# A 31-tap depthwise convolution moved wholly to TensorE: four time shifts stacked over the partitions, eight rounds of four 32-column products for each tile

## The chip, the cores and the metric

One core of one Trainium2 chip. The metric is the device time of the whole program in microseconds, median of three runs. A profile of one further execution gives every instruction of the core; all times below count from the start of its span.

## The reference, cut to what matters

The program is two networks in a row: two layers of a first block, then four layers of a second one. The change touches one part of one layer, the convolution module that opens the second network. It works on 256 tokens (T) and 1024 channels (D):

```python
def causal_dwconv(x, w, b):                      # w: 31 taps x 1024 channels
    xp = jnp.pad(x, ((0, 0), (width - 1, 0), (0, 0)))
    ...                                          # each channel with its own 31 taps
    return y + b

def conformer_conv_module(h, w_pw1, b_pw1, dw_w, dw_b, ln_g, ln_b, w_pw2, b_pw2):
    # u = GLU(h @ w_pw1 + b_pw1)
    u = causal_dwconv(u, dw_w, dw_b)
    # layer norm over the channels, silu, @ w_pw2 + b_pw2
```

All of it is float32.

## The kernel before, in words

Channels lie on the 128 partitions and time along the free axis, so 1024 channels are eight tiles (KD) of 128 x 256. The function `conformer` builds the stage.

**The projection.** `project` computes h @ w_pw1 on TensorE (PE). Each weight block of 128 x 128 takes three products (lines 761, 762, 763), because both operands are split in a rounded upper part and a rest. Step m of the eight steps makes the two tiles (value and gate) of output tile m: 16 blocks, 48 products. Steps 0 and 1 are made together at the start (`open_step`). Weights come as units of 1 MB through a ring of six units, loaded by SyncE (SP, line 494, called from `Weights.refill`), which waits until a unit has been used. ScalarE (ACT, line 563) rounds each chunk of weights and VectorE (DVE, line 572) subtracts to get the rest. `act_step` and `dve_step` do that some chunks ahead.

**The gate.** When step m is done, ACT evicts the value (line 2608) and the sigmoid of the gate (2609), and DVE multiplies them into `u[:, m]` and raises `glu_ready` (2653).

**The convolution.** Tiles 3, 5 and 7 are convolved on PE: 31 products for each tile, one for a tap, with a 128 x 128 diagonal matrix of that tap's weights as the stationary operand and the shifted window of `u` as the moving one (line 2674, plain float32: two records in the trace for each product). ACT makes these 93 diagonals (line 2612) and takes the finished tile out of PSUM (`take`, line 2598, signal `conv_taken`). Tiles 0, 1, 2, 4 and 6 are convolved on DVE, one instruction for a tap and tile (lines 2627 and 2629, 155 in all), between its pieces of weight work and, what is left, after the last gate.

**What follows.** `statistics` sums the eight tiles on PE with a matrix of ones (line 2688, `mean_ready`). DVE subtracts the mean (line 2662), ACT squares (2621), PE sums the squares (2692). Just ahead of that, ACT splits one more chunk of weights for the next projection and loads a table (lines 563 and 816), and DVE takes the rest of that chunk (572).

**Elsewhere in the program** stand products whose stationary operand has fewer than 128 columns. Lines 2960, 2961 and 2962 issue, in turn, products of 96, 64 and 32 moving columns, each with a 128 x 32 stationary block and each to another group of 32 PSUM partitions. Lines 1950 and 1953 issue products with 64 stationary columns to alternate halves of the PSUM partitions, two on one half, then two on the other. All are plain float32.

Of the kernel before, what the change touches and what calls it, by code (L numbers as in the profile page):

```python
# [13 lines left out]
ALU = mybir.AluOpType  # L14
ACT = mybir.ActivationFunctionType
AX = mybir.AxisListType

P = 128
T = 256
NT = T // P  # L20
D = 1024
KD = D // P
# [43 lines left out]
ARENA_CUTS = (8192, 16384, 26624)  # L66
BANK = 512

MAGIC = 12582912.0
# [244 lines left out]
def parameter_columns():  # L314
    c = Columns()
# [22 lines left out]
    c.add("b_pw1", "cc_b_pw1_2", (0,), 2 * KD)  # L338
    c.add("dw_w", "cc_dw_w_2", (0,), TAPS_CC * KD)
    c.add("dw_b", "cc_dw_b_2", (0,), KD)  # L340
# [20 lines left out]
def shape_constants():  # L361
# [8 lines left out]
        "right_angle": np.where((p >= D_NOPE) & (p < D_QK), np.pi / 2, 0.0),  # L370
        "ident": p == f,
        "heads": p // D_RW == f // D_RW,
        "causal_add": np.concatenate([np.zeros((P, P)), np.where(f <= p, 0.0, NEG)], 1),
# [289 lines left out]
def over(ap, n):  # L663

    ap = ap.unsqueeze(1)
    return ap.broadcast_to([ap.shape[0], n] + list(ap.shape[2:]))
# [14 lines left out]
def project(chip, st, name, nk, epilogue, x=None, rhs=None, per=1, x_ready=None, entry=None, after=None, free=None,  # L681
            inserts=None, depth=None):

# [16 lines left out]
    @block.sync  # L700
    def _(sp):
        w.refill(sp, chip.groups[name])

# [1834 lines left out]
def conformer(chip, i):  # L2538
# [6 lines left out]
    xs = chip.x[:, :].rearrange("p (c t) -> p c t", t=T)  # L2545
    pad = TAPS_CC - 1
    u = chip.place(4 * SLOT, KD, pad + T)
    conv, plain = chip.place(6 * SLOT, KD, T), slot2(chip, 12)
    squares, rstd = slot2(chip, 3), chip.stat[:, 3 * T:4 * T]
    e = [chip.place(7 * SLOT + b * T, T) for b in range(2)]  # L2550
    on_pe, on_dve = (3, 5, 7), ((0, 1), (2, 4), (6,))
    taps_of = lambda tiles: [(m, n) for m in tiles for n in range(TAPS_CC)]
    pe_taps = taps_of(on_pe)
    diagonals_by = (4, 8, 14, 20, 38, 56, 75, len(pe_taps))
    n_first = 2 * SLOT // P
    first, rest = chip.place(SLOT, n_first, P), chip.place(7 * SLOT + 2 * T, len(pe_taps) - n_first, P)
    diagonal = lambda c: first[:, c, :] if c < n_first else rest[:, c - n_first, :]
    tap = lambda m, n: chip.col("dw_w", n * KD + m)
    conv_bank = lambda c: chip.bank(6 + c % 2, T)
    half = TAPS_CC // 2  # L2560
    w = chip.weights

    with fused(chip) as st:
        whole_ready, upper_ready, lower_ready, glu_ready, conv_ready, conv_taken, diagonals_ready, taps_done, mean_ready, \
            centred, squared, var_ready, root_ready = st.signals(
                "whole_ready", "x_upper_ready", "x_lower_ready", "glu_ready", "conv_ready", "conv_taken", "diagonals_ready",
                "taps_done", "mean_ready", "centred", "squared", "var_ready", "root_ready")

# [21 lines left out]
        def glu(block, s, banks, steps):  # L2590

            @block.scalar
            def _(act):
                made = taken = 0

                def take(c):
                    act.wait_ge(conv_ready, c + 1)
                    act.activation(conv[:, on_pe[c], :], conv_bank(c), ACT.Identity,
                                   bias=chip.col("dw_b", on_pe[c])).then_inc(conv_taken, 1)

                for m in range(KD):
                    s["act_step"](act, m)
                    if m == 7:
                        take(0)
                    act.wait_ge(s["ready"], s["through"](m))
                    if m >= 2:
                        act.wait_ge(glu_ready, m - 1)
                    act.activation(u[:, m, pad:pad + T], banks(m)[0], ACT.Identity, bias=chip.col("b_pw1", m))
                    act.activation(e[m % 2], banks(m)[1], ACT.Sigmoid,
                                   bias=chip.col("b_pw1", KD + m)).then_inc(s["free"], 1)  # L2610
                    for tile, n in pe_taps[made:diagonals_by[m]]:
                        act.activation(diagonal(made), chip.con("ident"), ACT.Identity,
                                       scale=tap(tile, n)).then_inc(diagonals_ready, 1)
                        made += 1
                for c in range(1, len(on_pe)):
                    take(c)
                w.act(act, s["last"])
                load_roots(act)
                for k in range(KD):
                    act.wait_ge(centred, k + 1)  # L2620
                    act.activation(squares[:, k, :], conv[:, k, :], ACT.Square, scale=1.0 / 32).then_inc(squared, 1)
                act.wait_ge(var_ready, 1)
                root_of(chip, act, rstd, chip.bank(1, T), LN_EPS, root_ready)

            def convolve(dve, m, n):
                if n == 0:
                    return dve.tensor_scalar(conv[:, m, :], u[:, m, 0:T], tap(m, 0), chip.col("dw_b", m),
                                             ALU.mult, ALU.add)
                return dve.scalar_tensor_tensor(conv[:, m, :], u[:, m, n:n + T], tap(m, n), conv[:, m, :],  # L2629
                                                ALU.mult, ALU.add)  # L2630

            @block.vector
            def _(dve):
                chain = Chain(dve, s["dve_chain"])
                todo = [(m, n, pair) for pair in on_dve for n in range(TAPS_CC) for m in pair]
                state = {"taps": 0, "glus": 0}

                def take_taps(count):

                    for m, n, pair in todo[state["taps"]:state["taps"] + count]:  # L2640
                        if pair[-1] >= state["glus"]:
                            return
                        if n:
                            dve.wait_ge(taps_done, state["taps"] - len(pair) + 1)
                        convolve(dve, m, n).then_inc(taps_done, 1)
                        state["taps"] += 1

                w.between = lambda dve, c: take_taps(3 if state["glus"] < 4 else 9)
                dve.memset(u[:, :, 0:pad], 0.0)
                for m in range(KD):  # L2650
                    s["dve_step"](dve, m)
                    dve.wait_ge(s["free"], m + 1)
                    chain(dve.tensor_tensor(u[:, m, pad:pad + T], u[:, m, pad:pad + T], e[m % 2], ALU.mult), glu_ready)  # L2653
                    state["glus"] += 1
                w.between = lambda dve, c: None
                take_taps(len(todo))
                dve.wait_ge(taps_done, len(todo))
                w.dve(dve, s["last"])
                dve.wait_ge(conv_taken, len(on_pe))
                dve.wait_ge(mean_ready, 1)  # L2660
# [4 lines left out]

        def taps(pe, start, count):
            for c in range(start, start + count):
                m, n = pe_taps[c]
                if n == 0:
                    pe.wait_ge(glu_ready, m + 1)  # L2670
                    if c // TAPS_CC >= 2:
                        pe.wait_ge(conv_taken, c // TAPS_CC - 1)
                pe.wait_ge(diagonals_ready, c + 1)
                ins = pe.matmul(conv_bank(c // TAPS_CC), diagonal(c), u[:, m, n:n + T], start=(n == 0),  # L2674
                                stop=(n == TAPS_CC - 1))
                if n == TAPS_CC - 1:
                    ins.then_inc(conv_ready, 1)

        def statistics(pe):
            taps(pe, TAPS_CC + half, 2 * TAPS_CC - half)  # L2680
            ones = chip.con("ones")
            order = [m for pair in on_dve for m in pair] + list(on_pe)
            for k, m in enumerate(order):
                if m in on_pe:
                    pe.wait_ge(conv_taken, on_pe.index(m) + 1)
                else:
                    pe.wait_ge(taps_done, TAPS_CC * (k // 2 * 2 + len(on_dve[k // 2])))
                ins = pe.matmul(chip.bank(0, T), ones, conv[:, m, :], start=(k == 0), stop=(k == KD - 1))
            ins.then_inc(mean_ready, 1)
            for k in range(KD):  # L2690
# [3 lines left out]

        project(chip, st, ("pw1", i), KD, glu, per=2, x=h, x_ready=lower_ready, after=statistics, depth=3,
                inserts={10: lambda pe: taps(pe, 0, half), 12: lambda pe: taps(pe, half, TAPS_CC - half),
                         14: lambda pe: taps(pe, TAPS_CC, half)})

# [1126 lines left out]
```

## Time and profile before

| | |
|---|---|
| median of three runs | 2506.34 us (2505.02 to 2508.89) |
| the profiled execution's own time | 2506.61 us |
| its span, first to last instruction | 2504.8 us |
| mean granted TensorE clock | 0.971 |
| TensorE / VectorE / ScalarE busy over the span | 93% / 78% / 58% |
| the stage: first product of the projection to first subtraction of the mean | 976.3 to 1082.3 us |

The profile names a group of instructions by line, engine and operation, with the tile written, the tiles read and their shapes. The time an engine sat idle is put down to the instruction that ended it. A TensorE record's duration holds the latency of its pipeline, so the rate of products is read from starts, not from durations.

### The profile page before, as it was taken

The numbers are of one execution on the slowest core, as the hardware profiler recorded it, in microseconds if no ns is written. First come the engines' busy times: TensorE is split into PE (matmuls) and PEld (weight loads), VectorE is DVE, ScalarE is ACT, GpSimd is POOL, SyncE is SP. The second block draws the span as 40 slices with busy tenths as digits, with TensorE's granted clock in tenths as the row PEclk, the third lists the DMA queues.
The fourth block names the chain that finished last, engine by engine and source line by source line (L and its number), as shares of the span: only waits on it lengthen the run. The fifth ranks groups of instructions, "written<-read, shape, count | busy, mean of one in ns | idle before, by whom it ended". The sixth has DMA issues, their size and how long they took to land. (4 is left out here: it accounts for less than half of the span.)

```text
span 2504.8 us, 45660 instructions
## 1 busy us (share of the span) xinstructions
PE 2330.6 (93%) x18410; PEld 2221.1 (89%) x18410; DVE 1947.6 (78%) x3438; ACT 1447.1 (58%) x2673; POOL 12.8 (1%) x20
## 2 busy tenths in 40 slices
PE   8899999989999998889998979999988999988998
PEld 7899999978999998779997979997787999866998
DVE  6578798766688976968888868896559889857885
ACT  7535565465365645657746667656454775534764
POOL 0000000000000000000000000000000000000000
PEclk9999999999999999999999989999998999989999
DMA  6215577723175786214585525573425457722552
GB/s 248 89 52 203 189 285 299 303 85 120 50 256 206 285 320 228 85 68 169 192 311 221 202 93 179 201 286 135 169 84 185 167 189 304 272 97 89 197 186 101
DMA packets 64226, 463.36 MB, mean 185 GB/s; under 512 B 7248, under 2 KB 7440, under 8 KB 8208
## 3 DMA queue, kind: packets, MB, share of 16 engines
q1 hardware_dynamic: 64016, 460.44, 49.6%
q8 instruction: 146, 2.39, 0.4%
q14 instruction: 64, 0.52, 0.1%
HBM read 459.37 MB, written 1.05 MB: 184 GB/s over the span
## 5 line engine op out<-in xcount | busy, mean ns | idle before, releaser
L761 PE MATMUL psum<-arena_rounded,upper_rounded 128*128 128x256 f32 (+1 forms) x4792 | 1355.9, 283 | 75.8 <-DVE ring_rounded L572 22.2
L762 PE MATMUL psum<-arena_rounded,upper_rounded 128*128 128x256 f32 (+1 forms) x4792 | 1342.7, 280 | 0.0
L763 PE MATMUL psum<-arena_rounded,ring_rounded 128*128 128x256 f32 (+1 forms) x4792 | 1342.5, 280 | 0.0
L572 DVE TENSOR_TENSOR ring_rounded<-ring,upper_rounded 128x1024 fp32r<-128x1024 f32 (+4 forms) x958 | 838.3, 897 | 246.4 <-ACT upper_rounded L563 242.9
L563 ACT ACTIVATE upper_rounded<-ring 128x1024 fp32r<-128x1024 f32 (+4 forms) x958 | 751.0, 795 | 479.2 <-PE psum L763 385.6
L761 PEld LDWEIGHTS psum<-arena_rounded,upper_rounded 128*128 128x128 f32 (+1 forms) x4792 | 912.3, 190 | 93.8 <-issue 56.6
L762 PEld LDWEIGHTS psum<-arena_rounded,upper_rounded 128*128 128x128 f32 (+1 forms) x4792 | 910.6, 190 | 0.9 <-issue 0.5
L763 PEld LDWEIGHTS psum<-arena_rounded,ring_rounded 128*128 128x128 f32 (+1 forms) x4792 | 910.5, 190 | 0.0
L587 DVE CUSTOM_DVE_ANT_0 ring<-ring,silu_c,cols 128x1024 f32<-128x1024 f32 x192 | 244.7, 1279 | 0.0
L2502 DVE SCALAR_TENSOR_TENSOR arena<-psum,cols,arena 128x255 f32<-128x255 f32 (+1 forms) x352 | 153.2, 477 | 57.3 <-ACT arena L2469 54.2
L2469 ACT ACTIVATE arena<-psum,cols 128x256 f32<-128x256 f32 x176 | 89.5, 561 | 70.8 <-PE psum L763 68.7
L724 PE MATMUL psum<-arena_rounded,upper_rounded 128*128 128x256 f32 x320 | 82.0, 290 | 9.8 <-DVE ring_rounded L572 7.6
L725 PE MATMUL psum<-arena_rounded,ring_rounded 128*128 128x256 f32 x320 | 79.6, 283 | 0.0
L724 PEld LDWEIGHTS psum<-arena_rounded,upper_rounded 128*128 128x128 f32 x320 | 61.8, 193 | 13.4 <-DVE ring_rounded L572 6.1
L2629 DVE SCALAR_TENSOR_TENSOR arena<-arena,cols 128x256 f32<-128x256 f32 x150 | 63.6, 479 | 1.1
L725 PEld LDWEIGHTS psum<-arena_rounded,ring_rounded 128*128 128x128 f32 x320 | 61.9, 193 | 0.1
L2674 PE MATMUL psum<-arena 128*128 128x256 f32 x186 | 44.1, 398 | 9.8 <-DVE arena L2653 9.8
L729 PE MATMUL psum<-arena_rounded,upper_rounded 128*128 128x256 f32 x320 | 51.5, 284 | 0.1
L2674 PEld LDWEIGHTS psum<-arena 128*128 128x128 f32 x186 | 36.8, 200 | 16.0 <-DVE arena L2653 10.4
L2162 ACT ACTIVATE stat<-psum 128x256 f32<-128x256 f32 x64 | 24.2, 382 | 43.1 <-PE psum L763 40.7
L2315 ACT ACTIVATE arena_rounded<-x,small 128x256 fp32r<-128x256 f32 x56 | 33.7, 602 | 19.1 <-DVE x L2418 18.3
L729 PEld LDWEIGHTS psum<-arena_rounded,upper_rounded 128*128 128x128 f32 x320 | 43.7, 192 | 1.1 <-DVE arena_rounded L2411 1.1
(517 smaller groups left out, 2545.4 us busy)
## 6 DMA issues: line engine op xcount, KB each, us to landing
ring<-stream_dram SPq DMA_DIRECT2D x434, 1024.0 KB, 4.9
const<-const_dram SPq DMA_DIRECT2D x1, 1540.0 KB, 14.8
x<-x_dram SPq DMA_DIRECT2D x1, 1024.0 KB, 4.8
out_dram<-x SPq DMA_DIRECT2D x4, 256.0 KB, 2.0
cols<-cols_dram SPq DMA_DIRECT2D x1, 974.0 KB, 11.5
silu_c<-c_dram SPq DMA_DIRECT2D x1, 512.0 KB, 15.7
const<-const_dram SPq DMA_DIRECT2D x1, 67.0 KB, 4.6
pos<-positions_dram SPq DMA_DIRECT2D x1, 64.0 KB, 6.0
```

Of the source, the lines that this page charges most:

```text
L563: act.activation(self.chip.rounded(upper), raw, ACT.Identity).then_inc(self.upper_ready, 1)
L572: dve.tensor_tensor(self.chip.rounded(raw), raw, self.chip.whole(upper), ALU.subtract).then_inc(self.lower_ready, 1)
L587: dve.tensor_tensor_reduce(row, row, chip.silu_c[:, :], 1.0, chip.col(("ada_b", lead), which * KD + m), ALU.mult, ALU.add, chip.ada[:, col ...
L724: pe.matmul(out, upper, x[0][:, k, :], start=(k == 0), stop=False)
L725: pe.matmul(out, lower, x[0][:, k, :], start=False, stop=False)
L729: ins = pe.matmul(banks(b.tile // per)[b.tile % per][0:b.width], upper, x[1][:, k, :], start=False, stop=(k == nk - 1))
L761: pe.matmul(out, upper, x[0][:, b.k, :], start=(b.k == 0), stop=False)
L762: pe.matmul(out, upper, x[1][:, b.k, :], start=False, stop=False)
L763: ins = pe.matmul(out, lower, x[0][:, b.k, :], start=False, stop=(b.k == nk - 1))
L2469: ins = act.activation(conv[b][:, half, :], banks(m)[half], ACT.Identity, scale=tap(m, half, 2), bias=chip.col(("ffn_b", i), half * KF + m))
L2502: ins = dve.scalar_tensor_tensor(c[:, back:T], banks(m)[half][:, 0:T - back], tap(m, half, 2 - back), c[:, back:T], ALU.mult, ALU.add)
L2674: ins = pe.matmul(conv_bank(c // TAPS_CC), diagonal(c), u[:, m, n:n + T], start=(n == 0), stop=(n == TAPS_CC - 1))
```

## The change

The convolution leaves DVE and the 128 x 128 diagonals go. For each tile m:

- SP copies `u[:, m]` inside SBUF into `shifted[m]`, 16 transfers of 32 partitions x 284 elements: for each group q of 32 channels and each shift n of 0 to 3, the channels of q moved n places in time, at partitions 32n to 32n+31. SP does this in program order between its refills (`beside=shift` in `project`): refill of step m, wait for `glu_ready` m+1, 16 transfers, refill of step m+1 and so on.
- DVE builds all diagonals of a tile in one instruction of 128 x 1024 (`build`), in one of four buffers, right behind the gate's product.
- PE computes eight rounds (taps 4r to 4r+3) of four products (one for each group of 32 channels). The stationary operand is 128 x 32, the moving one 128 x 256, and product q writes PSUM partitions 32q to 32q+31. Tile m for m = 0 to 4 is put in front of step m+3 of the projection; tiles 5, 6 and 7 come behind the projection, with the sums of the mean between.
- ACT takes all eight tiles out of PSUM, the first ones in front of the eviction of step m+4.

```diff
+QUAD = 32
+GROUPS_CC, ROUNDS_CC = P // QUAD, -(-TAPS_CC // (P // QUAD))
...
     @block.sync
     def _(sp):
-        w.refill(sp, chip.groups[name])
+        at = 0
+        for step in range(steps if beside else 0):
+            to = max(n for n, b in enumerate(chip.groups[name]) if not b.side and b.tile // per == step) + 1
+            w.refill(sp, chip.groups[name][at:to])
+            at = max(at, to)
+            beside(sp, step)
+        w.refill(sp, chip.groups[name][at:])
...
                 for m in range(KD):
                     s["act_step"](act, m)
-                    if m == 7:
-                        take(0)
+                    if m > lag:
+                        take(m - lag - 1)
...
-                    for tile, n in pe_taps[made:diagonals_by[m]]:
-                        act.activation(diagonal(made), chip.con("ident"), ACT.Identity,
-                                       scale=tap(tile, n)).then_inc(diagonals_ready, 1)
-                        made += 1
-                for c in range(1, len(on_pe)):
-                    take(c)
+                for m in range(KD - lag - 1, KD):
+                    take(m)
...
+                def build(m):
+                    if m >= ahead:
+                        dve.wait_ge(conv_ready, m - ahead + 1)
+                    dve.tensor_tensor(diagonals[m % ahead],
+                                      chip.col("dw_w", m * n_blocks, n_blocks).unsqueeze(2).broadcast_to([P, n_blocks, QUAD]),
+                                      over(chip.con("quads"), n_blocks), ALU.mult).then_inc(diagonals_ready, 1)
+
                 dve.memset(u[:, :, 0:pad], 0.0)
+                dve.memset(u[:, :, pad + T:], 0.0)
                 for m in range(KD):
                     s["dve_step"](dve, m)
                     dve.wait_ge(s["free"], m + 1)
                     chain(dve.tensor_tensor(u[:, m, pad:pad + T], u[:, m, pad:pad + T], e[m % 2], ALU.mult), glu_ready)
-                    state["glus"] += 1
-                w.between = lambda dve, c: None
-                take_taps(len(todo))
-                dve.wait_ge(taps_done, len(todo))
+                    build(m)
...
+        def taps(pe, m):
+            pe.wait_ge(shifted_ready[m], 16 * n_transfers)
+            pe.wait_ge(diagonals_ready, m + 1)
+            if m >= 2:
+                pe.wait_ge(conv_taken, m - 1)
+            for r in range(ROUNDS_CC):
+                for q in range(GROUPS_CC):
+                    ins = pe.matmul(chip.psum[QUAD * q:QUAD * (q + 1), conv_bank(m) * BANK:conv_bank(m) * BANK + T],
+                                    diagonals[m % ahead][:, q * ROUNDS_CC + r, :],
+                                    shifted[m][:, q, GROUPS_CC * r:GROUPS_CC * r + T],
+                                    start=(r == 0), stop=(r == ROUNDS_CC - 1))
+            ins.then_inc(conv_ready, 1)
+
+        def shift(sp, m):
+            sp.wait_ge(glu_ready, m + 1)
+            for n in range(GROUPS_CC):
+                for q in range(GROUPS_CC):
+                    sp.dma_start(shifted[m][QUAD * n:QUAD * (n + 1), q, :],
+                                 u[QUAD * q:QUAD * (q + 1), m, n:n + reach]).then_inc(shifted_ready[m], 16)
...
+            taps(pe, KD - lag)
+            for k in range(KD - lag - 1):
+                add_to_mean(k)
+            taps(pe, KD - 2)
+            add_to_mean(KD - 4)
+            taps(pe, KD - 1)
+            for k in range(KD - lag, KD):
+                ins = add_to_mean(k)
...
+        project(chip, st, ("pw1", i), KD, glu, per=2, x=h, x_ready=lower_ready, after=statistics, depth=3, beside=shift,
+                inserts={2 * (m + lag): lambda pe, m=m: taps(pe, m) for m in range(KD - lag)})
```

`lag` is 3, `ahead` is 4, `n_blocks` is 32 and `n_transfers` is 16. The table of tap weights is laid out anew on the host and one constant of 32 columns is added.

## Rows read from the trace of the kernel before

**Rows 1.** The page, busy time of each engine over the span.
```profile
PE 2330.6 (93%) x18410; PEld 2221.1 (89%) x18410; DVE 1947.6 (78%) x3438; ACT 1447.1 (58%) x2673; POOL 12.8 (1%) x20
```
**Rows 2.** Busy time by stretch; after the engines the granted clock, DMA share, GB/s.
```profile
995.00:1005.00 10.00, 8.84 (x63) 8.84 (x64) 9.97 (x20) 7.00 (x18) 0.00 (x0) 0.83 0.36 125
...
1045.00:1055.00 10.00, 8.46 (x46) 7.24 (x44) 9.97 (x24) 7.87 (x23) 0.00 (x0) 1.00 0.31 105
1055.00:1065.00 10.00, 2.83 (x7) 2.29 (x8) 9.75 (x23) 0.00 (x0) 0.00 (x0) 0.64 0.00 0
1065.00:1075.00 10.00, 10.00 (x41) 8.51 (x40) 9.32 (x20) 0.00 (x0) 0.00 (x0) 0.85 0.01 2
```
**Rows 3.** Groups by line, 985 to 1085 us: busy, mean ns, idle before.
```profile
L2629 DVE SCALAR_TENSOR_TENSOR arena<-arena,cols 128x256 f32<-128x256 f32 x150 | 63.6, 479 | 1.1
L2674 PE MATMUL psum<-arena 128*128 128x256 f32 x186 | 44.1, 398 | 9.8 <-DVE arena L2653 9.8
...
L2612 ACT ACTIVATE arena<-const,cols 128x128 f32<-128x128 f32 x93 | 28.0, 395 | 0.0
```
**Rows 4.** Timeline of DVE: start, length, line, idle before.
```profile
990.50 0.43 DVE L2653 TENSOR_TENSOR arena<-arena 128x256 f32<-128x256 f32 x1 [3.10 <-ACT arena L2609]
...
1062.15 15.07 DVE L2629 SCALAR_TENSOR_TENSOR arena<-arena,cols 128x256 f32<-128x256 f32 x29
1080.27 1.23 DVE L572 TENSOR_TENSOR ring_rounded<-ring,upper_rounded 128x1024 fp32r<-128x1024 f32 x1 [3.05 <-ACT upper_rounded L563]
1082.28 2.74 DVE L2662 SCALAR_TENSOR_TENSOR arena<-psum,arena 128x256 f32<-128x256 f32 x8 [0.78 <-PE psum L2688]
```
**Rows 5.** Timeline of PE, two products of the projection, then the stage's end.
```profile
999.92 0.28 PE L761 MATMUL psum<-arena_rounded,upper_rounded 128*128 128x256 f32 x1
...
1005.70 0.28 PE L761 MATMUL psum<-arena_rounded,upper_rounded 128*128 128x256 f32 x1
...
1062.17 16.54 PE L2674 MATMUL psum<-arena 128*128 128x256 f32 x62 [8.72 <-DVE arena L2653]
1078.55 3.62 PE L2688 MATMUL psum<-arena,const 128*128 128x256 f32 x16
```
**Rows 6.** Groups by line, PE from 1430.5 us: products with 32 stationary columns.
```profile
L2960 PE MATMUL psum<-arena 128*32 128x96 f32 x32 | 2.8, 247 | 0.0
```
**Rows 7.** Busy time in the stretch of lines 2960 to 2962.
```profile
1430.56:1433.14 2.58, 2.58 (x96) 2.58 (x96) 2.55 (x4) 2.52 (x3) 0.00 (x0) 1.00 0.00 0
```
**Rows 8.** Timeline of PE: products with 64 stationary columns.
```profile
187.84 0.44 PE L1950 MATMUL psum<-arena 128*64 128x128 f32 x4
188.06 0.43 PE L1953 MATMUL psum<-arena 128*64 128x128 f32 x4
```
**Rows 9.** Timeline of SP: issues of transfers, length and count.
```profile
2.12 0.55 SPq L934 DMA_DIRECT2D pos<-positions_dram  x1
2.71 0.58 SPq L494 DMA_DIRECT2D ring<-stream_dram  x1
...
988.21 0.33 SPq L494 DMA_DIRECT2D ring<-stream_dram  x1
...
1383.97 1.28 SPq L494 DMA_DIRECT2D ring<-stream_dram  x3
```
**Rows 10.** The page's issues of transfers: count, KB each, us to landing.
```profile
ring<-stream_dram SPq DMA_DIRECT2D x434, 1024.0 KB, 4.9
...
out_dram<-x SPq DMA_DIRECT2D x4, 256.0 KB, 2.0
```
**Rows 11.** Timeline of ACT.
```profile
988.22 0.48 ACT L2608 ACTIVATE arena<-psum,cols 128x256 f32<-128x256 f32 x1 [1.81 <-PE psum L763]
988.70 1.28 ACT L2609 ACT_TABLE_LOAD   x1
...
1079.12 1.05 ACT L563 ACTIVATE upper_rounded<-ring 128x1024 fp32r<-128x1024 f32 x1
```
**Rows 12.** DVE instructions of 128 x 1024 by shape, whole span.
```profile
L2896 DVE TENSOR_TENSOR arena<-arena 128x1024 f32<-128x1024 f32 x8 | 9.8, 1223 | 1.8 <-ACT arena L2880 1.8
```

More of the change, by code:

```diff
@@ L338, in parameter_columns @@
     c.add("b_pw1", "cc_b_pw1_2", (0,), 2 * KD)
-    c.add("dw_w", "cc_dw_w_2", (0,), TAPS_CC * KD)
+    c.add("dw_w", "cc_dw_w_2", (0,), KD * GROUPS_CC * ROUNDS_CC, "shifted")
     c.add("dw_b", "cc_dw_b_2", (0,), KD)
@@ L371, in shape_constants @@
         "ident": p == f,
+        "quads": (p % QUAD == f)[:, 0:QUAD],
         "heads": p // D_RW == f // D_RW,
@@ L681, in project @@
 def project(chip, st, name, nk, epilogue, x=None, rhs=None, per=1, x_ready=None, entry=None, after=None, free=None,
-            inserts=None, depth=None):
+            inserts=None, depth=None, beside=None):
     w, block = chip.weights, st.block
@@ L2545, in conformer @@
     xs = chip.x[:, :].rearrange("p (c t) -> p c t", t=T)
-    pad = TAPS_CC - 1
-    u = chip.place(4 * SLOT, KD, pad + T)
+    pad, reach = TAPS_CC - 1, T + GROUPS_CC * (ROUNDS_CC - 1)
+    u = chip.place(4 * SLOT, KD, reach + GROUPS_CC)
     conv, plain = chip.place(6 * SLOT, KD, T), slot2(chip, 12)
@@ L2550, in conformer @@
     e = [chip.place(7 * SLOT + b * T, T) for b in range(2)]
[L2551 to L2560, printed above, removed]
+    shifted = [chip.place(7 * SLOT + 2 * T + m * GROUPS_CC * reach, GROUPS_CC, reach) for m in range(KD)]
+    n_blocks = GROUPS_CC * ROUNDS_CC
+    ahead = 2 * SLOT // (n_blocks * QUAD)
+    diagonals = [chip.place(SLOT + m * n_blocks * QUAD, n_blocks, QUAD) for m in range(ahead)]
+    conv_bank = lambda m: 6 + m % 2
+    lag = 3
     w = chip.weights
+    n_transfers = GROUPS_CC * GROUPS_CC
     with fused(chip) as st:
[L2564 to L2567, printed above, removed]
+        whole_ready, upper_ready, lower_ready, glu_ready, conv_ready, conv_taken, diagonals_ready, mean_ready, \
+            centred, squared, var_ready, root_ready, *shifted_ready = st.signals(
+                "whole_ready", "x_upper_ready", "x_lower_ready", "glu_ready", "conv_ready", "conv_taken",
+                "diagonals_ready", "mean_ready", "centred", "squared", "var_ready", "root_ready",
+                *(f"shifted_ready_{m}" for m in range(KD)))
         @st.block.scalar
@@ L2593, in _, with take @@
             def _(act):
[L2594 to L2599, printed above, removed]
+                def take(m):
+                    act.wait_ge(conv_ready, m + 1)
+                    act.activation(conv[:, m, :], chip.bank(conv_bank(m), T), ACT.Identity,
+                                   bias=chip.col("dw_b", m)).then_inc(conv_taken, 1)
                 for m in range(KD):
                     s["act_step"](act, m)
-                    if m == 7:
-                        take(0)
+                    if m > lag:
+                        take(m - lag - 1)
                     act.wait_ge(s["ready"], s["through"](m))
@@ L2623, in _ @@
                 root_of(chip, act, rstd, chip.bank(1, T), LN_EPS, root_ready)
[L2625 to L2630, printed above, removed]
             @block.vector
@@ L2634, in _ @@
                 chain = Chain(dve, s["dve_chain"])
[L2635 to L2648, printed above, removed]
+                def build(m):
[4 more added lines that the diff above has]
+                                      over(chip.con("quads"), n_blocks), ALU.mult).then_inc(diagonals_ready, 1)
                 dve.memset(u[:, :, 0:pad], 0.0)
+                dve.memset(u[:, :, pad + T:], 0.0)
                 for m in range(KD):
@@ L2653, in _ @@
                     chain(dve.tensor_tensor(u[:, m, pad:pad + T], u[:, m, pad:pad + T], e[m % 2], ALU.mult), glu_ready)
-                    state["glus"] += 1
-                w.between = lambda dve, c: None
-                take_taps(len(todo))
-                dve.wait_ge(taps_done, len(todo))
+                    build(m)
                 w.dve(dve, s["last"])
-                dve.wait_ge(conv_taken, len(on_pe))
                 dve.wait_ge(mean_ready, 1)
@@ L2664, in glu @@
             return "act dve"
[L2666 to L2677, printed above, removed]
+        def taps(pe, m):
[10 more added lines that the diff above has]
+            ins.then_inc(conv_ready, 1)
@@ L2679, in statistics @@
+        def shift(sp, m):
[4 more added lines that the diff above has]
+                                 u[QUAD * q:QUAD * (q + 1), m, n:n + reach]).then_inc(shifted_ready[m], 16)
         def statistics(pe):
-            taps(pe, TAPS_CC + half, 2 * TAPS_CC - half)
             ones = chip.con("ones")
-            order = [m for pair in on_dve for m in pair] + list(on_pe)
@@ L2683, in statistics, with add_to_mean @@
[L2683 to L2688, printed above, removed]
+            def add_to_mean(k):
+                pe.wait_ge(conv_taken, k + 1)
+                return pe.matmul(chip.bank(0, T), ones, conv[:, k, :], start=(k == 0), stop=(k == KD - 1))
@@ L2693, in statistics @@
             ins.then_inc(var_ready, 1)
-        project(chip, st, ("pw1", i), KD, glu, per=2, x=h, x_ready=lower_ready, after=statistics, depth=3,
-                inserts={10: lambda pe: taps(pe, 0, half), 12: lambda pe: taps(pe, half, TAPS_CC - half),
-                         14: lambda pe: taps(pe, TAPS_CC, half)})
+        project(chip, st, ("pw1", i), KD, glu, per=2, x=h, x_ready=lower_ready, after=statistics, depth=3, beside=shift,
+                inserts={2 * (m + lag): lambda pe, m=m: taps(pe, m) for m in range(KD - lag)})
     def out(st):
@@ L3803 @@
             cols[:, at] = np.concatenate([a[0:D_NOPE]] + [a[lo:hi] for lo, hi in turned(D_NOPE)])
+        elif rows == "shifted":
+            for r in range(TAPS_CC):
+                part = cols[QUAD * (r % GROUPS_CC):QUAD * (r % GROUPS_CC + 1), at + r // GROUPS_CC:at + n:ROUNDS_CC]
+                part[:] = a[r].reshape(-1, QUAD).T
         elif rows is None:
```

## The prediction

> **What bounds the kernel now.** I read the page first: TensorE is busy 93% of the span [rows 1], so elsewhere a microsecond off another engine is worth nothing. The stage is the exception. The busy times by stretch show PE falling to 8.5 and then 2.8 of 10 us from 1045 to 1065 while DVE stays at 9.8 to 10, and the granted clock down at 0.64 and 0.85 [rows 2]. The groups by line say what DVE does: 150 tap instructions, 63.6 us; ACT spends 28.0 us on 93 diagonals [rows 3]. The timelines show the end. PE waits 8.72 us for the last gate, which stands in DVE's order behind taps, then runs tile 7's 31 taps in 16.54 us; DVE's own last 29 taps end at 1077.2. The eight sums of the mean run from 1078.55, and the subtraction of the mean starts at 1082.28 [rows 4, 5]. That instant is my yardstick. Behind it the same work follows in both kernels, so the gain is 1082.28 less its new time.
>
> **PE's new work.** A plain float32 product of 256 columns takes (3.62 - 0.17 of latency at the end) / 8 = 0.43 us [rows 5]. Were the 32 products of a tile run one behind the other, that is 13.9 us; run four at a time, 8 x 0.43 = 3.45 us. Which holds? Lines 2960 to 2962 go to three groups of 32 PSUM partitions. At 0.43 us for 256 columns, 16 triples of 96 + 64 + 32 columns in series would take 5.2 us, and the 96-column ones alone 2.6 us. All 96 records lie in 2.58 us [rows 6, 7]. The groups overlap, and the shorter ones cost nothing. Lines 1950 and 1953 agree: four records of 128 columns start within 0.22 us where one alone needs 0.107 [rows 8], twice the rate, though two products in a row go to the same half. So order doesn't forbid overlap. But both places deliver just two streams' worth on average; four equal full streams are not shown. I take four at a time, nearest to the three lines which didn't slow each other, with 0.2 us for passing between the forms: 3.65 us a tile. The bounds are 7.1 us (two at a time) and 14.1 us (none).
>
> The Trainium skill, "TensorE: Matmul & The Clock Gate", Part 3 (measured speedup against the span model), speaks partly against this: four tiles of the array at once gave 3.07 times, three column tiles 2.38 times. By 3.07 a tile would take 4.7 us and the subtraction start some 6 us later than by 3.65. No row here shows four.
>
> **SP's new work** is 128 transfers. Three issues in a row took 1.28 us, (1.28 - 0.33) / 2 = 0.47 us from start to start, a single one being 0.33 long; at the program's start it was 0.59 (2.12 to 2.71) [rows 9]. No row shows a copy inside SBUF of 32 rows. Bounds 0.38 and 0.60 us; I take 0.47, the row in the middle of the run. A tile is then 15 x 0.47 = 7.05 us from first to last issue, 7.5 in SP's time. The landing I take as 2.0 us, like the 256 KB stores; a 1 MB unit takes 4.9 and stands ahead in the same queue, but its issue is 7 us older by the last copy [rows 10].
> **Walking the new order.** Steps 0 and 1 end at 988.1 [rows 11]. A projection product takes (1005.70 - 999.92) / 51 = 0.1133 us [rows 5], a step of 48 thus 5.44.
> - Step 2 ends at 993.5, and PE comes to tile 0's taps. But gate 0 ends only at 990.93 (ACT first loads a table, 1.28 us) [rows 4, 11]. SP issues from 991.0, the last at 998.05, landed 1000.05. **PE stalls 6.5 us.**
> - The clock: after the 8.7 us stall the granted clock was 0.64 and 0.85 in two stretches [rows 2, 5]. The 62 records then took 16.54 us where 62 x 0.217 is 13.4, a loss of 3.0; in the stretch from 995 the 0.83 cost 1.7. Both are time at 1.2 GHz in place of 2.4. I take 2.2. Tile 0 ends at 1005.9.
> - Steps 3 to 7 are 27.2; taps 1 to 4 are 14.6. Taps 2, 3 and 4 wait for the take-out of the tile two before, which ACT does just ahead of the step's eviction: I give 0.3 each. The projection ends at 1048.6.
> - SP meanwhile: copy 1 ends by 1006 and is wanted at 1011; copies 2 to 6 each stay 1 to 10 us ahead. SP in one piece, 991.0 + 8 x 7.5 + 7 refills x 0.5, would be done at 1054.5, so it isn't the bound, by little.
> - Behind the projection: taps 5 (3.65), four sums (1.7), taps 6 (3.65), one sum (0.4) end at 1058.0. Gate 7 takes 1.8 us after its step (2.8 at tile 0, less the table, plus a take-out), so 1050.4; last copy issued 1057.55, landed 1059.55. A second stall, 1.55 us, with half a chance of the 1.7 clock loss: 0.85. Taps 7 end at 1064.05.
> - Then ACT's take-out (0.25 latency, 0.37 until the next can start), its 1.05 us weight chunk, and DVE's 1.23 us on that chunk with 0.1 between, before it may subtract [rows 4, 11]: 3.0 us. Before, these two lay beside the eight sums; now only three are left, so they come on the path. Subtraction starts at **1067.05, gain 15.2 us**.
>
> **Costed at nothing.** The 155 DVE taps go, off a path that is now PE's and SP's; the 93 ACT diagonals too. DVE's eight builds are 1.22 us each [rows 12], 9.8 us where 65 went, each needed 5 us or more later. With build 0 ahead of the small weight chunk of step 2, that chunk is ready about 992.5, just before PE wants it at 992.8: if late, the 6.5 us stall swallows it. Refills of weights come up to 12 us later than now, as SP stands at gates and issues copies. The ring has five units, 27 us and more, in hand, and DMA moved nothing from 1055 to 1075 [rows 2], so it hides that. The added columns and the memset are under 0.3 us.
>
> The sum is against the profiled execution, 2506.6 us (span 2504.8 and 1.8 around it), 0.3 above the median: 2506.3 - 15.2 = **2491 us**.
>
> **The rivals.**
> 1. *Copies dearer or later.* At 0.55 us an issue SP is the chain: 991 + 70.4 + 3.5 + 1.45 to the last landing = 1066.35, then taps, clock (1.7) and tail 8.35: 1074.7, gain 7.6. At 0.60: 1081, gain 1. For: the 0.59 row; SP has 2 us of slack. Against: it was cold start. 2494 to 2506.
> 2. *Copies cheaper.* At 0.38: first stall 1.35 shorter, no second: gain 18.8. With no stall at all: 6.55 + 2.2 + 1.55 + 0.85 = 11.2 more, gain 26.4, 2480. For: the transfers are small, 36 KB. Against: the single issue alone is 0.33.
> 3. *The other side: only two column groups run at a time.* A tile costs 7.1 us, PE is the chain throughout, 1000.05 + 8 x 7.1 + 2.2 + 27.2 + 0.9 + 2.1 + 3.0 = 1092.3: 10 us slower, 2516. It decides from 5.85 us a tile on. For: the two rates measured are both exactly two streams. Against: the 32-column products were free beside the other two.
> 4. *No overlap*, the change doesn't do what it says: 14.1 us a tile, 1148, 66 us slower, 2572. Against: [rows 6 to 8] outright.
>
> **Chances.** Forecast (2486 to 2496) 0.55; rival 1 0.18; rival 2 below 2486 0.10; rival 3 0.13; rival 4 0.04. The range 2482 to 2505 leaves out 3 and 4 and the last of 2. A difference under 0.2%, 5 us, can't be told from none. Faster 0.80 (forecast, rival 2, most of 1), same 0.05 (rival 1 near 0.60), slower 0.15.
>
> **What would show it.** The new product line should lie in stretches of 3.5 us for 64 records at full clock; 7 says rival 3. PE idle before the first of them 6 to 7 us, released by a transfer, and the last 1 to 2. SP starts 0.47 apart, 16 in a row. DVE half idle from 1000 to 1060. PE's clock below 1 after 1000. The weight chunk (L572) should be what stands right ahead of the subtraction. Wrong it would be made above all by the four-fold overlap, then by the issue time, where 0.1 us is 13 us of SP.

## The result and the profile after

The changed kernel takes 2545.74 us (median of 4 runs, 2542.11 to 2547.37) against 2507.61 us for the kernel before, run beside it: ratio 1.0147, 95% interval 1.0126 to 1.0169. It is 38 us slower; 2491 us and a gain of 15 were forecast. The profiled span is 2542.4 us against 2504.8, 37.6 us more.

The first reading is where those 37.6 us lie. I cut each trace at two instants that both kernels have, the stage's first projection product and its first subtraction of the mean. Before, they are at 976.33 and 1082.28, after at 987.00 and 1102.54. The stage went from 105.95 to 115.54 us, +9.6. The other 28.0 us lie outside it, 10.7 ahead and 17.3 behind, where no instruction was meant to change.

**Inside the stage.** Page of the changed kernel, issues of transfers (the third column is us to landing):

```profile
arena<-arena SPq DMA_DIRECT2D x128, 35.5 KB, 1.9
```

Timeline of SP, changed kernel:

```profile
1003.20 21.34 SPq L2668 DMA_DIRECT2D arena<-arena  x32
1024.58 0.58 SPq L497 DMA_DIRECT2D ring<-stream_dram  x1
1025.20 11.10 SPq L2668 DMA_DIRECT2D arena<-arena  x16
1036.35 0.58 SPq L497 DMA_DIRECT2D ring<-stream_dram  x1
...
1082.12 10.54 SPq L2668 DMA_DIRECT2D arena<-arena  x16
```

SP is never free from 1003.20 to 1092.66. Sixteen copies take 10.0 to 11.2 us. Their starts are mostly 0.633 us apart; five of the eight tiles hold one issue that takes 1.3 to 1.7 us instead, so the average in the row from 1025.20 is 0.70 ((11.10 - 0.59) / 15) and over all 128 copies 0.67 (89.46 us less six refills of 0.62, by 128). A copy behind another holds SP for 0.59 us, where the issue in [rows 9] that follows a wait took 0.33. With the refill behind it a tile costs 11.4 us of SP on average.

What PE waited for, 985 to 1130 us (us in total, times, longest), and the stretches of PE (busy time by engine, then the granted clock):

```profile
PE psum L2658 <- DMA arena<-arena: 21.8, 6, 7.8
```
```profile
1010.00:1020.00 10.00, 5.37 (x52) 2.57 (x56) 1.43 (x2) 0.00 (x0) 0.00 (x0) 0.50 0.21 53
...
1080.00:1090.00 10.00, 7.01 (x66) 3.12 (x66) 0.00 (x0) 0.47 (x1) 0.00 (x0) 0.66 0.50 158
1090.00:1100.00 10.00, 6.04 (x65) 2.85 (x66) 0.00 (x0) 0.05 (x1) 0.00 (x0) 0.66 0.08 22
```

DVE and ACT are almost idle there, the reverse of [rows 2]; PE waits for copies and then runs at half the clock. A copied tile's taps were short when the clock was full. The stretch from tile 1's first record to past the start of its last one, counting only line 2658:

```profile
1026.72:1030.12 3.40, 3.39 (x64) 1.98 (x64) 1.00 0.89 337
```

64 records in 3.4 us: the four column groups run side by side. And DVE at the stage's end shows the weight chunk right ahead of the subtraction, where [rows 4] had a wait for PE:

```profile
1101.40 1.22 DVE L575 TENSOR_TENSOR ring_rounded<-ring,upper_rounded 128x1024 fp32r<-128x1024 f32 x1 [26.24 <-ACT upper_rounded L566]
1102.54 2.73 DVE L2647 SCALAR_TENSOR_TENSOR arena<-psum,arena 128x256 f32<-128x256 f32 x8
```

**Outside the stage.** Over some stretches of the trace, as from 340 to 417 us, like instructions of the two kernels drift apart by 0.64 us in each 16.3 us of projection; over others, as from 823 to 960 us, not at all. So I counted products in a stretch where both kernels do nothing but weight projection, 350 to 400 us, long before the change. The count in brackets behind PE's busy time is what to read. Before, then after:

```profile
350.00:400.00 50.00, 50.00 (x444) 50.00 (x443) 45.73 (x82) 30.73 (x64) 0.00 (x0) 1.00 0.75 279
```
```profile
350.00:400.00 50.00, 50.00 (x427) 50.00 (x427) 43.66 (x79) 29.68 (x63) 0.00 (x0) 1.00 0.74 273
```

PE is busy throughout and at full clock in both, yet issues 444 products in one and 427 in the other: 112.6 and 117.1 ns each by this count. Over the whole trace the gaps between starts of products of lines 761 to 763 (770 to 772 after) fall into two heaps, near 113.3 and 117.8 ns. Before, 60% of some 13,900 gaps were in the lower one, mean 115.11 ns; after, 13%, mean 117.22. The difference times 13,900 is 29 us, the 28 us looked for. No instruction was changed there; addresses were: the longer tables `cols` and `const` pushed the arena 128 bytes on, from 64 to 192 past a multiple of 256.

### The profile page after: what moved, and what is told of

It is laid out like the page before. It is cut to its first block and busy times, and to the rows that moved or that the text cites. A ratio compares the mean times of both kernels' runs of the same rounds, so it can differ in the third digit from the quotient of the medians.

```text
span 2542.4 us, 46205 instructions
## 1 busy us (share of the span) xinstructions
PE 2360.7 (93%) x18736; PEld 2236.3 (88%) x18736; DVE 1895.3 (75%) x3292; ACT 1420.5 (56%) x2585; POOL 12.8 (1%) x20
## 5 line engine op out<-in xcount | busy, mean ns | idle before, releaser
L2658 PE MATMUL psum<-arena 128*32 128x256 f32 x512 | 38.6, 468 | 22.7 <-DMA arena<-arena 21.8
L2658 PEld LDWEIGHTS psum<-arena 128*32 128x32 f32 x512 | 19.2, 133 | 40.2 <-DMA arena<-arena 24.5
L2287 ACT ACTIVATE stat<-x,small 128x256 f32<-128x256 f32 x64 | 36.0, 577 | 11.8 <-DVE x L2341 10.2
```

What stands on the lines that cost most here:

```text
L2658: ins = pe.matmul(chip.psum[QUAD * q:QUAD * (q + 1), conv_bank(m) * BANK:conv_bank(m) * BANK + T], diagonals[m % ahead][:, q * ROUNDS_CC + ...
```

## The experiments

Theory Q: SP's issues set the stage. Theory P: the tensors' placement sets the spacing of all products of the program. Rivals: slow copying; a spacing that any edit draws anew. "Stage" is first product to first subtraction in the trace, "outside" the rest of the span.

**1 and 2 (e1, e2). The place alone, both ways.**

```diff
 # e1, on the kernel before: addresses of the changed kernel, its instructions those of before
         self.cols = sb("cols", columns.n)
+        sb("room_a", 8)
         self.const = sb("const", sum(n for _, n in constants.values()))
+        sb("room_b", 32)
 # e2, on the changed kernel: the arena another 128 bytes on
-        begin_at_multiple_of(128, 64)
+        begin_at_multiple_of(256, 64)
```

> The kernel before with two unused columns blocks, so that every tensor behind cols lies where the changed kernel has it (the arena 128 bytes higher); no instruction differs. Outside the convolution stage the changed kernel lost 28 us, all of it in products of the weight projections that start 117.8 ns apart in place of 113.3 ns. Theory P (placement): where the tensors lie sets that spacing; then this is 25 to 30 us slower than before, about 2535 us, and nearly all products are 117.8 ns apart. Rival R (the spacing is drawn anew at each restart of TensorE and so follows from any edit): no fixed direction, and with not one instruction changed rather the same as before, 2507 us +-5.

Measured: 2532.66 us, ratio 1.0098 (1.0076 to 1.0120), outside 2424.1 us where the kernel before has 2398.9. Not an instruction changed, and it lost 25 us. "Nearly all" was too much: 76% of its gaps lie in the upper heap (87% in the changed kernel), mean 116.7 ns. All but 1.4 us of its loss came behind the stage, where the changed kernel lost 10.7 ahead of it: in these two traces the place sets the share, not which stretch is slow.

> The changed kernel with its arena moved on by another 128 bytes, to the same remainder by 256 bytes as before the change. Theory P: the products return to 113.3 ns in about the share that they had before, and of the 38 us some 28 come back: 2518 us. Rival R: no fixed direction, 2545 +-10. If the share of the two spacings stays as in the changed kernel, arena placement is not the cause.

Measured: 2519.04 us, ratio 1.0029 (1.0012 to 1.0046), outside 2399.6 us, stage 114.3, 67% of the gaps in the lower heap, mean 114.8 ns. Placement accounts for 25 us one way (e1) and 27 of the 38 us the other (e2). The kernel before spread over 2494.9 to 2523.6 us in its 68 executions, and none of e1's (from 2532.2) falls within that. With the arena back, what is left of the change is +8.4 us in the stage and a ratio of 1.0029.

**3 and 4 (e3, e4). SP's issues.**

```diff
 # e3, half the issues, same bytes
-            for n in range(GROUPS_CC):
+            for n in range(2):
                 for q in range(GROUPS_CC):
-                    sp.dma_start(shifted[m][QUAD * n:QUAD * (n + 1), q, :],
-                                 u[QUAD * q:QUAD * (q + 1), m, n:n + reach]).then_inc(shifted_ready[m], 16)
+                    sp.dma_start(shifted[m][64 * n:64 * (n + 1), q, :],
+                                 u[64 * (q // 2):64 * (q // 2 + 1), m, n:n + reach]).then_inc(shifted_ready[m], 16)
 # e4, shared with GpSimd; PE waits for both signals
+        @st.block.gpsimd
+        def _(pool):
+            for m in range(KD):
+                shift(pool, m, (2, 3), chip.by_pool)
```

> The changed kernel with 8 transfers of 64 partitions for a tile in place of 16 of 32: the same bytes and the same waits, other data, so the convolution's output is not the reference's. Theory Q (SyncE's issues set the stage's end: 16 x 0.68 + 0.6 us is 11.4 us a tile against 9.1 of TensorE's work): the stage falls to TensorE's pace, 8 x 5.4 + 0.6 = 6.0 us of issues a tile, first stall 3 to 5 us in place of 8, and the subtraction of the mean starts 18 to 25 us earlier, seen from the stage's first product. Rival B (the copying itself, bytes or landing, is slow): no gain in the stage, under 3 us.

Measured: stage 86.9 us, 28.6 less than the changed kernel. 2514.91 us, ratio 1.0024 (1.0004 to 1.0045), the placement still bad (outside 2422.5). The bytes are the same, so the copying was not slow; rival B falls. The gain was larger than expected (18 to 25), as the cold restarts went too: all eight tiles' taps ran at a granted clock of 1.00, where in the changed kernel tiles 0, 4, 6 and 7 had 0.56 to 0.68.

> The changed kernel with half of each tile's copies (shifts 2 and 3) issued by GpSimd, the other half by SyncE; all results stay the reference's. Theory Q: SyncE needs 8 x 0.68 + 0.6 = 6.0 us a tile; if a GpSimd issue costs up to 1.1 us the stage is TensorE's and ends 15 to 22 us earlier than in the changed kernel. Rival B: no gain. If GpSimd's issues take over 1.4 us each, it is the new bound and the stage is no shorter.

Measured: stage 86.7 us, 28.9 less; 2516.91 us, ratio 1.0025 (1.0008 to 1.0041), outside 2435.2 (its profiled execution was its slowest, 2523.66 us, with 5% of the gaps in the lower heap). POOL's and then SP's timeline of this kernel:

```profile
1028.21 3.91 POOL L2670 DMA_DIRECT2D arena<-arena  x8 [5.45 <-DVE arena L2643]
```
```profile
1012.77 4.97 SPq L2670 DMA_DIRECT2D arena<-arena  x8
...
1027.95 5.87 SPq L2670 DMA_DIRECT2D arena<-arena  x8
1035.72 0.33 SPq L498 DMA_DIRECT2D ring<-stream_dram  x1
1037.78 5.43 SPq L2670 DMA_DIRECT2D arena<-arena  x8
```

GpSimd issues every 0.49 us, SP now rests between tiles, and the stage is 19.3 us shorter than before the change. Theory Q holds.

**5 (e5). Both causes removed:** e4 and, on it,

```diff
-        begin_at_multiple_of(128, 64)
+        begin_at_multiple_of(256, 64)
```

> SyncE and GpSimd share the copies, and the arena lies at 64 bytes past a multiple of 256, as in the kernel before. If the two causes are apart and add up: the stage takes 87 us as with the shared copies (106 before), the rest of the program is as before, so 2509 - 19 = 2490 us, faster than before by 0.8%. If sharing the queues had moved the product spacing by itself, it stays near 2515.

Measured: 2492.70 us, ratio 0.9937 (0.9917 to 0.9958); stage 87.9, outside 2399.1. The two causes add, and this beats the kernel before by 0.6%.

**6 to 10 (e6, e7, e9, e10, e12). Which place?** All are the kernel before with one or two of these lines changed, `room` standing ahead of the ring. Their expectations follow in the order e6, e7, e9, e10, e12:

```diff
+        sb("room", 32)
         self.ring = sb_rounded_too("ring", RING * UNIT)
-        begin_at_multiple_of(128, 64)
+        begin_at_multiple_of(256, 0)   # or 64, 128, 192
```

> The kernel before, its arena alone moved, from 64 to 0 bytes past a multiple of 256. Theory P says that only the place of the moving operand by 256 bytes counts; 0 has not been seen. If 64 is special, 0 is slower: 2520 to 2570 us; if only 192 is bad, 2509.

> The kernel before, its arena alone moved by 128 bytes to 192 past a multiple of 256; the small tensors stay where they were. Theory P (the arena's place does it): about 2533 us, like the run in which everything behind cols was moved. Rival: it was the small tensors, then 2509.

> The kernel before, its arena alone moved from 64 to 128 bytes past a multiple of 256. So far 64 gave 2507 us, 192 2534 and 0 2548. If the even multiples of 64 are the dear ones, about 2548 us again; if 128 is as good as 64, 2507.

> The kernel before, with everything in front of the arena (the ring of weights, their upper parts, x) moved by 128 bytes and the arena still 64 past a multiple of 256. If the arena's own place sets the spacing of the products, 2507 us; if it is the distance between the stationary operand's place (ring, upper) and the moving one's (arena), then as with the arena at 192, 2534 us.

> The kernel before with the tensors in front of the arena moved by 128 bytes, as in the last run of this kind, and the arena moved by 128 bytes as well (192 past a multiple of 256). Each of the two moves alone made it 2534 us. If the distance between the two operands' places by 256 bytes sets the spacing of the products, they cancel: 2507 us. If each place counts by itself, it stays at 2534 or gets worse.

| arena past a multiple of 256 | ring, upper, x | mean gap of products, ns | outside, us | median us | ratio (95%) |
|---|---|---|---|---|---|
| 64, the kernel before | as before | 115.1 | 2398.9 | 2507.61 | |
| 192 (e7) | as before | 117.3 | 2430.4 | 2534.33 | 1.0097 (1.0069 to 1.0125) |
| 0 (e6) | as before | 118.7 | 2440.9 | 2548.12 | 1.0158 (1.0133 to 1.0184) |
| 128 (e9) | as before | 119.9 | 2460.5 | 2568.94 | 1.0247 (1.0230 to 1.0265) |
| 64, 256 bytes on (e10) | 128 bytes on | 117.1 | 2427.0 | 2534.55 | 1.0112 (1.0096 to 1.0127) |
| 192 (e12) | 128 bytes on | 114.9 | 2403.9 | 2506.96 | 0.9980 (0.9951 to 1.0009) |

Each ratio is against the kernel before run beside it. The stage was 106.0 to 106.6 us in all of them. The same stretch of pure projection, arena at 128 and then both moved:

```profile
350.00:400.00 50.00, 50.00 (x419) 50.00 (x419) 44.05 (x80) 28.89 (x61) 0.00 (x0) 1.00 0.74 279
```
```profile
350.00:400.00 50.00, 50.00 (x444) 50.00 (x443) 45.89 (x82) 31.08 (x65) 0.00 (x0) 1.00 0.74 274
```

e7 clears the small tensors: moving the arena alone costs all of it. e10 and e12 show that it is no property of the arena's own address: moving the front alone costs the same 27 us, and moving both costs nothing. It is the distance, by 256 bytes, between the arena and the tensors in front of it, where the stationary operand lies. The ring and the upper parts start 128 bytes past a multiple of 256 (at 0 in e10 and e12), so that distance is 192 before and in e12, 64 in e7 and e10, 128 in e6 and 0 in e9, the slowest. That a whole 256 bytes make no difference rests on e2. All tensors in front were moved together, so that the stationary operand is the one that counts is not shown. e6 came out within its range and e7 as Theory P said; e9 fitted neither of its values. In e6 and e9 the two heaps are gone too: in e6 the gaps spread from 114 to 123 ns, in e9 95% are 120 ns.

**11 (e8). The order of the 32 products,** on e4:

```diff
-            for r in range(ROUNDS_CC):
-                for q in range(GROUPS_CC):
+            for q in range(GROUPS_CC):
+                for r in range(ROUNDS_CC):
```

> Shared copies, and the 32 products of a tile in another order: all eight of one column group, then all eight of the next. If the overlap of the column groups needs neighbours in the order that go to different groups, a tile takes 13.7 us in place of 3.4 and the stage grows by 8 x 10 us; if TensorE looks far enough ahead (16 records and their loads), it takes between 3.4 and 7 us.

Measured: stage 152.2 us where e4 has 86.7; one execution only, 2583.83 us. One tile's stretch, only its products:

```profile
1028.00:1039.20 11.20, 11.18 (x64) 5.90 (x64) 1.00 0.48 148
```

64 records in 11.1 us: neither value was right. It is 2.6 us better than in series (64 x 0.213, an estimate), 7.7 worse than by rounds. Within a group the starts lie 0.216 us apart; only at each of the three changes of group do some follow by 6 or 30 ns. By rounds three of every four starts follow by 7 ns.

**12 (e11). The first stall,** on e5:

```diff
-    lag = 3
+    lag = 4
...
-            taps(pe, KD - lag)
-            for k in range(KD - lag - 1):
+            for m in range(KD - lag, KD - 2):
+                taps(pe, m)
+            for k in range(KD - 4):
```

> Shared copies, placed arena, and every tile's convolution one step later (lag 4 in place of 3). With lag 3 TensorE still waits 3.0 us for tile 0's copies and runs some 2 us of it at half the clock. Theory Q: a step more covers that; TensorE's work is the same, so the stage is 3 to 5 us shorter, 83 to 85 us, and the run 2487 to 2490. Rival: the last tiles' tail grows by what the front gains, then 2493 as with lag 3.

Measured: 2487.81 us, ratio 0.9929 (0.9907 to 0.9951), stage 84.1. What PE's new product waited for, from the groups by line, 985 to 1104 us:

```profile
L2660 PE MATMUL psum<-arena 128*32 128x256 f32 x512 | 29.1, 380 | 1.7 <-ACT arena L2605 1.7
```

No wait for a copy is left, and 3.8 us came back as expected. In the whole time it can't be told from e5, whose interval covers it. It is the fastest version of the study.

## Why the prediction was wrong, point by point

- **The issue time, the failed step inside the stage.** "Bounds 0.38 and 0.60 us; I take 0.47" was measured at 0.63 us for most copies and 0.67 on average. I had the 0.59 row in hand [rows 9] and set it aside as a cold start; the 0.47 came from issues with a wait between. SP's slack was 2 us in my own sum, and 16 x 0.20 us a tile broke it. By rival 1's formula, 991 + 128 x 0.67 + 3.7 (six refills) + 1.3 + 8.35 is 1090 against 1082.28, +8; the stage grew 9.6, 8.4 with the arena back. So the mechanism was named, and its upper bound stopped 0.07 us short of the truth. e3 and e4 show it. The trace before had more rows of issues with no wait between, at its start, and they would not have settled it:

```profile
3.81 0.43 SPq L937 DMA_DIRECT2D cols<-cols_dram  x1
4.28 0.44 SPq L938 DMA_DIRECT2D const<-const_dram  x1
4.77 0.44 SPq L939 DMA_DIRECT2D silu_c<-c_dram  x1
```

The twelve gaps between starts at the beginning of that trace run from 0.45 to 0.65 us, mean 0.52. A wait in between is only part of it: in e4, after 1.7 us of rest, a copy held SP 0.51 us and a refill of weights 0.33. So a copy inside SBUF was dearer to issue than the loads that I priced it by; why is open.
- **"Behind it the same work follows in both kernels"**, and added columns "under 0.3 us": the work was the same and its speed was not. This took 28 us and no rival had it: it is the larger of the two failed steps. e1, e2, e7, e10 and e12 show it. Without it (e2) the change is still slower, by a ratio of 1.0029 (1.0012 to 1.0046), where 15 us of gain were forecast; that rest is the issue time above.
- **Four column groups at once: right.** 3.4 us a tile where 3.45 and 0.2 were written. The Trainium skill's 3.07 times ("TensorE: Matmul & The Clock Gate", Part 3) is for four row tiles of 512 columns, its 2.38 for three column tiles. For four column tiles of 256 columns this trace gives, as an estimate, 13.7 / 3.4, four times. "Order doesn't forbid overlap" was only half right: e8 lost 7.7 us a tile to order, and the change's own order by rounds is what earns the overlap.
- **The first stall**: 6.5 us written. It was 7.8, with the dearer issues; after it the taps took 6.0 us in place of 3.4, a clock loss of 2.7 where 2.2 stood. At 2.0 us the landing was right (1.9).
- **"Copies 2 to 6 each stay 1 to 10 us ahead": wrong.** Two waits for copies were written, 8.1 us in all; six came, 21.8 us: 7.8 before tile 0, 1.4, 1.9 and 2.1 before tiles 2 to 4, 4.4 and 4.2 before tiles 6 and 7 (the tail, where 1.55 stood). The granted clock was 0.56 to 0.68 over the taps of tiles 0, 4, 6 and 7, which took 9.3 us more together than at full clock; 3.05 was written.
- **DVE and ACT off the path, the chunk right ahead of the subtraction: right.** With SP relieved the stage took 86.7 us, 19.3 less than before, where 15.2 were forecast. That is no test of the forecast's own figure: eight issues of 0.64 us a tile are 5.1 us, less than sixteen of 0.38, for which rival 2 gave 18.8. The walk, given its issues, was about right.

## What to carry to other kernels

When a change adds many small transfers, price the issue by rows of the same kind of transfer, one behind the other with no wait between, and, where the trace has none, by the dearest row (here 0.45 to 0.65 us before, 0.67 after), and compare the queue's whole time with the stage before anything else; if it is near the bound, share it between two queues. When a change adds or lengthens a tensor, everything behind it moves: count the products in a stretch that the change doesn't touch, and fix the placement (here by one aligned start) before judging the change. A loop over column groups should go round them, not through them one by one.

## What the runs showed of the hardware that I had not expected

The gap between like 128 x 128 x 256 products depends on the distance by 256 bytes between the arena, where the moving operand lies, and the tensors in front of it, the stationary operand's among them: mean gaps 115, 117, 119 and 120 ns at distances of 192, 64, 128 and 0, 61 us of this program between best and worst. At 192 and 64, within one kernel, both gaps of 113.3 and 117.8 ns occur with no tensor moved, in stretches that start and end at short pauses of TensorE (113.3 until 417 us in the trace before, where one step is longer, then 117.8). What passes there is open: I did not find why the distance weights the one or the other, nor whether stationary or moving reads lose, nor whether a distance that is no multiple of 64 bytes would hold it at 113.3 throughout. The lowest share of slow gaps seen was 23%, in e5.

How long an issue holds SP depends on the transfer and on what stands ahead of it. After a rest of 1.5 to 2.4 us a copy inside SBUF of 32 rows took 0.51 us (e4), one of 64 rows 0.46 (e3), a 1 MB refill of 128 rows 0.33. Right behind another issue a copy took 0.59 (32 rows) or 0.60 (64 rows; e3's starts are mostly 0.639 apart), a refill 0.58 behind a copy and 0.43 behind another refill (trace before, 1384.34 us). GpSimd's copies were 0.49 apart.
